# The sample streams of an attention stage follow each other every fourth unit in place of every sixth

## The chip, the cores and the metric

The kernel runs on one core of a Trainium2 chip. The metric is the time of one execution in microseconds of device time; of several runs the median counts.

## The reference

One layer of a streaming encoder. A combined input projection feeds two groups of heads, a retention mixer and an attention with a learned index; both go through an output projection, a normalization and a feed-forward block. There are two inputs: a prompt of 1024 frames, and 8 running streams ("samples") with 16 new frames each, which see 256 cached keys beside their own. The part that the change touches is the attention, for the prompt and for the samples alike:

```python
score = jnp.where(admissible[None], score, -jnp.inf)
sel_score, sel = lax.top_k(score, n_sel)
k_sel = gather(k, sel)
v_sel = gather(v, sel)
logits = jnp.einsum('bqgrd,bqkgd->bqgrk', qg, k_sel).astype(jnp.float32) * (HD ** -0.5)
logits = jnp.where(valid[:, :, None, None, :], logits + bias, -jnp.inf)
p = jax.nn.softmax(logits, axis=-1)
out = jnp.einsum('bqgrk,bqkgd->bqgrd', p.astype(v.dtype), v_sel)
```

The kernel doesn't gather. It adds a mask to the logits of all keys, so a key that isn't selected gets no weight.

## The kernel before

The kernel goes through index scores, retention, attention, output projection and the two halves of the feed-forward block. In each stage every engine has a program of its own, written out in order; the engines wait for each other through semaphores. So the order of an engine's instructions is the order in the code, and an instruction that waits holds everything behind it on its engine.

The attention stage (`attention_programs`, L1511) has 64 units, one for each of 8 tiles of 128 queries and 8 heads: unit u is tile u // 8, head u % 8. All engines loop over u. At unit u TensorE forms the logits of unit u (`qk_u`, L1957), transposes the probabilities of unit u-2 (`turn_u`, L1968) and multiplies those of unit u-3 with the values (`pv_u`, L1984). VectorE adds mask and bias and finds the largest value (`logits`, L1803 and L1809), ScalarE takes the exponential (`exps`, L1732) and copies the transposed probabilities out of the PSUM (`keeps`, L1741). A tile t has t + 1 blocks of 128 keys, so units become longer with t. At every eighth unit the queries of the next tile are turned (`queries_turn`, L1906).

The eight sample streams are woven into these units. Stream s has six steps, at six units in a row, and `stream_at(u, step)` (L1575) says which stream, if any, has that step at unit u:

- Step 0: TensorE waits for the stream's cached keys and values (`c_in`), then transposes the keys (`keys_turn`, L1912 and L1913); ScalarE copies them (`keep_keys`, L1708 and L1709).
- Step 1: TensorE forms the logits and adds the mask (`qk_s`, L1924 and L1926); VectorE reduces them (`logits_s`, L1770).
- Steps 2 and 3: ScalarE takes the exponential (`exp_s`, L1714); VectorE inverts the sum (`invert_s`, L1775).
- Step 4: TensorE transposes the probabilities (`turn_s`, L1932); ScalarE copies them (`keep_probs_s`, L1722 and L1724).
- Step 5: TensorE multiplies them with the values (`pv_s`, L1943); VectorE scales the result (`out_s`, L1782); SyncE stores it.

On TensorE the order in a unit is: turned queries, `qk_u`, `keys_turn`, `qk_s`, `turn_u`, `turn_s`, `pv_s`, `pv_u`. On ScalarE it is: kept queries, `keep_keys`, `keeps`, `exps`, `exp_s`, `keep_probs_s`. On VectorE the logits of the unit come first, then `logits_s`, `invert_s` and `out_s`.

Keys and values of a stream lie in `kp` and `vp`, which have two buffers each, buffer s % 2 for stream s. The first two streams are loaded ahead of the stage. After that SyncE's program (`sync`, L1654) does the following at a unit that holds step 5 of stream s:

```python
sp.wait_ge(s_o, s + 1)
for h in range(HEADS):
    sp.dma_start(mix[r0:r0 + NEW, 512 + 64 * h:576 + 64 * h],
                 os_[h * NEW:(h + 1) * NEW, s % 2, :]).then_inc(s_out[s % 2], 16)
if s + 2 < NS:
    caches_in(sp, s + 2)
```

`s_o` counts the outputs of `out_s`. The eight stores are L1676; `caches_in` (L1627) issues a load of 128 KB of keys and one of 128 KB of values (L1633), and both count on the semaphore for which `keys_turn` waits. On the same queue stand, in the order of the units, the query and key rows of the next tiles (`queries_in`, L1624 and L1625, at units 5, 13, 21 and so on), the output projection's weights (L1670, at units 8, 10, 16, 18, 24, 26, 32 and 34, which wait for GpSimd from unit 16 on) and the stores of a finished tile (L1683, at units 10, 18, 26 and so on).

The PSUM banks for transposes, stream logits and stream outputs are three, taken in turn; the list of their uses is built from `stream_at`, so it follows any change there.

Of the kernel before, what the change touches and what calls it, by code (L numbers as in the profile page):

```python
# [278 lines left out]


RING = 12
STREAM_START, STREAM_GAP = 2, 6


class WeightRing:
# [2972 lines left out]
```

## Time and profile before

| | before |
|---|---|
| median of 3 runs | 1518.24 us (1518.0 to 1518.44) |
| the profiled execution's own time | 1519.36 us |
| its span | 1517.6 us |
| TensorE busy | 1455.2 us, 96% of the span |
| VectorE, ScalarE, GpSimd busy | 66%, 50%, 53% |
| mean granted clock of TensorE | 0.987 |

A busy share is an average over all stages. What a change in the attention stage is worth is read from the rows of that stage, which lies between about 490 and 663 us.

### The profile page before, as it was taken

How to read it: one execution, taken by the hardware profiler on the slowest of the kernel's cores; microseconds unless marked ns; L12 is line 12 of the kernel's file. 1: busy time of each engine (PE TensorE's matmuls, PEld its weight loads, DVE VectorE, ACT ScalarE, POOL GpSimd, SP SyncE). 2: the span in 40 equal slices, each digit the busy share in tenths (PEclk: the TensorE clock that was granted, in tenths of full speed). 3: DMA queues.
4: the chain of work that ended last, by engine and by line, in shares of the span. 5: the costliest groups of instructions: out<-in, count | busy, mean ns of one | idle time of the engine just before them, and what ended most of it. 6: DMA issues, size and time to landing. Idle time of an engine off the chain costs nothing.

```text
span 1517.6 us, 23208 instructions
## 1 busy us (share of the span) xinstructions
PE 1455.2 (96%) x7764; PEld 1214.9 (80%) x7764; DVE 1001.4 (66%) x1892; ACT 755.1 (50%) x1550; POOL 807.0 (53%) x685
## 2 busy tenths in 40 slices
PE   7998999999998899999999999999999999999995
PEld 6986787877777789988878888888887888888874
DVE  5368577777876654423459666566669777777787
ACT  5467477777676777634343334333344332332332
POOL 3310356656542343002456556546558977877888
PEclk9999899999999999999999999999999999999998
DMA  7310312121108451114322433433356444444344
GB/s 229 86 37 12 101 34 66 51 54 39 51 29 180 109 145 34 44 63 153 122 96 87 163 110 136 163 124 144 142 193 238 164 139 147 156 139 155 106 157 166
DMA packets 123886, 172.99 MB, mean 114 GB/s; under 512 B 46424, under 2 KB 95992, under 8 KB 121592
## 3 DMA queue, kind: packets, MB, share of 16 engines
q1 hardware_dynamic: 119840, 140.02, 30.1%
q10 hardware_dynamic: 3928, 31.48, 5.1%
q8 instruction: 63, 1.03, 0.3%
q14 instruction: 55, 0.45, 0.1%
HBM read 119.59 MB, written 51.88 MB: 113 GB/s over the span
## 4 chain that ended last, share of the span: by engine, by line
PE 60%; DVE 3%; POOL 3%; ACT 2%; issue 2%; SPq 1%; DMA 0%; POOLq 0%; ACTq 0%; DVEq 0%
PE wide L389 10%; PE wide L390 10%; PE wide L391 10%; PE paired L389 7%; PE paired L390 7%; PE paired L391 7%; PE paired L1984 4%; PE wide L1957 2%; PE paired L1968 2%; POOL acc L3044 1%; POOL acc L3053 1%; PE paired L2272 0%; DVE qT L1837 0%; DVE ob_mT_lo L2360 0%; SPq L1625 0%
## 5 line engine op out<-in xcount | busy, mean ns | idle before, releaser
L2169 POOL TENSOR_TENSOR wu_lo<-raw_u,wu_hi 128x512 fp32r<-128x512 f32 x64 | 97.0, 1529 | 148.1 <-ACT wu_hi L2164 148.1
L389 PE MATMUL paired<-w_hi,aT_hi 128*128 128x512 f32 x320 | 132.2, 413 | 1.4 <-PEq L424 1.4
L391 PE MATMUL paired<-w_hi,aT_lo 128*128 128x512 f32 x320 | 126.4, 395 | 0.0
L390 PE MATMUL paired<-w_lo,aT_hi 128*128 128x512 f32 x320 | 126.0, 394 | 0.0
L374 POOL TENSOR_TENSOR w_lo<-stage,w_hi 128x512 fp32r<-128x512 f32 (+1 forms) x50 | 64.4, 1303 | 99.2 <-ACT w_hi L369 99.2
L3083 DVE TENSOR_TENSOR acc<-wide,acc 128x512 f32<-128x512 f32 x116 | 79.5, 687 | 45.4 <-PE wide L391 45.2
L1070 ACT ACTIVATE spare<-scores,sl_key 128x768 bf16<-128x768 f32 (+2 forms) x96 | 100.1, 1043 | 11.3 <-DVE sl_key L1176 3.8
L389 PE MATMUL paired<-aT_hi,wu_hi 128*128 128x512 f32 x240 | 95.1, 396 | 1.5 <-DVE acc L3083 1.2
L2169 POOL TENSOR_TENSOR wu_lo<-w_sum,wu_hi 128x512 fp32r<-128x512 f32 x60 | 96.5, 1638 | 0.0
L390 PE MATMUL paired<-aT_lo,wu_hi 128*128 128x512 f32 x240 | 93.6, 390 | 0.0
L391 PE MATMUL paired<-aT_hi,wu_lo 128*128 128x512 f32 x240 | 93.6, 390 | 0.0
L3013 POOL TENSOR_TENSOR aT_lo<-t_sum,aT_hi 128x512 fp32r<-128x512 f32 x52 | 78.1, 1531 | 27.2 <-ACT aT_hi L2918 27.2
L1199 DVE TENSOR_SCALAR_CACHE_REDUCE spare<-scores,sl_key 128x384 bf16<-128x384 f32 (+3 forms) x128 | 86.8, 678 | 4.6
L1867 POOL TENSOR_TENSOR near<-bias,scores 128x2048 f32<-128x2048 f32 (+1 forms) x8 | 34.3, 4292 | 91.1 <-DVE mn L1809 69.9
L2936 ACT ACTIVATE aT_hi<-w_all 128x1792 fp32r<-128x1792 f32 x16 | 27.2, 1698 | 98.2 <-PE wide L391 98.2
L2586 DVE TENSOR_TENSOR f_out<-f_out 128x512 f32<-128x512 f32 (+1 forms) x48 | 49.4, 1029 | 39.8 <-ACT f_out L2563 32.6
L389 PEld LDWEIGHTS paired<-w_hi,aT_hi 128*128 128x128 f32 x320 | 60.4, 189 | 18.1 <-issue 5.0
L1984 PE MATMUL paired<-vt,pT 128*128 128x64 f32 x576 | 72.8, 272 | 1.0 <-ACT pT L1741 0.6
L1984 PEld LDWEIGHTS paired<-vt,pT 128*128 128x128 f32 x576 | 69.8, 193 | 2.4 <-ACT pT L1741 1.2
L391 PEld LDWEIGHTS paired<-w_hi,aT_lo 128*128 128x128 f32 x320 | 60.2, 188 | 14.0
L390 PEld LDWEIGHTS paired<-w_lo,aT_hi 128*128 128x128 f32 x320 | 60.4, 189 | 11.4
L2336 POOL TENSOR_SCALAR ob_st<-ob_st 128x1 f32<-128x1 f32 x18 | 3.4, 191 | 124.0 <-ACT ob_junk L2297 112.5
(393 smaller groups left out, 4732.3 us busy)
## 6 DMA issues: line engine op xcount, KB each, us to landing
f_scratch<-f_out ACTq DMA_DIRECT2D x15, 1984.0 KB, 6.1
w_all<-f_scratch SPq DMA_DIRECT2D x32, 896.0 KB, 4.8
raw_u<-in_w_up SPq DMA_DIRECT2D x16, 1024.0 KB, 5.4
raw_d<-in_w_down SPq DMA_DIRECT2D x16, 1024.0 KB, 7.1
stage<-in_w_in SPq DMA_DIRECT2D x32, 256.0 KB, 3.4
stage<-mix_scratch SPq DMA_DIRECT2D x9, 512.0 KB, 4.0
h_scratch<-ob_h SPq DMA_DIRECT2D x9, 512.0 KB, 2.9
fn_h<-h_scratch SPq DMA_DIRECT2D x9, 512.0 KB, 7.8
```

The source lines that it names most:

```text
L374: self.nc.gpsimd.tensor_tensor(lo, raw, hi.bitcast(F32), ALU.subtract).then_inc(self.lo_done, 1)
L389: nc.tensor.matmul(out, lhs[0], rhs[0], start=first, stop=False, skip_group_check=onto)
L390: nc.tensor.matmul(out, lhs[0], rhs[1], start=False, stop=False, skip_group_check=onto)
L391: return nc.tensor.matmul(out, lhs[1], rhs[0], start=False, stop=last, skip_group_check=onto)
L1070: nc.scalar.activation(act_junk[:, 0:P * (t + 1)], score[t][:], ACT.Sign, scale=-1.0, bias=limit, accum_out=c_sum[:, n:n + 1]).then_inc(sl ...
L1199: nc.vector.tensor_scalar(dve_junk[:, 0:cells.shape[1]], cells, limit, None, ALU.is_ge, ALU.add, accum_out=c_sum[:, n:n + 1]).then_inc(sl_ ...
L1867: nc.gpsimd.tensor_tensor(near[:, t % 2, :, 2 * P - w:], bias[:, :, 2 * P - w:], repeated(mask[t][:, P * (t + 1) - w:], 1, HEADS), ALU.add ...
L1984: mm = nc.tensor.matmul(po[:, h * HD:(h + 1) * HD], pT[:, n % 3, k * P:(k + 1) * P], vt[:, k0 + k, 64 * g:64 * g + 64], start=(k0 + k == 0 ...
L2169: self.nc.gpsimd.tensor_tensor(self.room.wu[1][:, s], self.source(i), self.room.wu[0][:, s].bitcast(F32), ALU.subtract).then_inc(self.lo_d ...
L2586: nc.vector.tensor_tensor(out, x, y, op).then_inc(marked, 1)
L3013: op = nc.gpsimd.tensor_tensor(s[1][:, n], x[:, n], s[0][:, n].bitcast(F32), ALU.subtract)
L3083: nc.vector.tensor_tensor(cells, bank, cells, ALU.add).then_inc(added, 1)
```

## The change

`STREAM_GAP` is the distance of two streams in units. It goes from 6 to 4. Stream s then begins at unit 2 + 4s in place of 2 + 6s, and ends at 7 + 4s in place of 7 + 6s; the last stream ends at unit 35, in the fifth tile, in place of unit 49, in the seventh. Steps 4 and 5 of stream s come to stand in the same units as steps 0 and 1 of stream s + 1. The load of the caches of stream s + 2 stands at unit 4s + 7 on SyncE, and the step that needs them at unit 4s + 10; before, these were 6s + 7 and 6s + 14.

```diff
 RING = 12
-STREAM_START, STREAM_GAP = 2, 6
+STREAM_START, STREAM_GAP = 2, 4
```

`STREAM_GAP` is used in one place:

```python
def stream_at(u, step):
    s, rest = divmod(u - STREAM_START - step, STREAM_GAP)
    return s if rest == 0 and 0 <= s < NS else None
```

## Rows read from the trace of the kernel before

**Rows 1.** Windows: us; busy (count) of PE, PEld, DVE, ACT, POOL; clock; DMA share; GB/s.

```profile
499.00:662.00 163.00, 155.04 (x1263) 139.85 (x1262) 82.10 (x282) 117.09 (x284) 46.07 (x15) 1.00 0.29 76
500.00:510.00 10.00, 8.45 (x71) 7.11 (x72) 6.70 (x27) 6.97 (x29) 4.56 (x1) 1.00 0.04 8
```

**Rows 2.** Waits of PE, 485 to 665 us: us in total, times, longest.

```profile
PE paired L1943 <- issue: 2.1, 3, 1.0
```

**Rows 3.** Timeline of SyncE's DMA queue: start, us, line, DMA, count.

```profile
504.28 3.57 SPq L1676 DMA_DIRECT2D mix_scratch<-os  x8
...
509.17 0.47 SPq L1633 DMA_DIRECT2D vp<-in_cache_v  x1
...
511.83 4.23 SPq L1625 DMA_DIRECT2D krow<-out  x1
516.11 4.20 SPq L1676 DMA_DIRECT2D mix_scratch<-os  x8
...
539.83 3.67 SPq L1676 DMA_DIRECT2D mix_scratch<-os  x8
...
544.03 0.47 SPq L1633 DMA_DIRECT2D vp<-in_cache_v  x1
...
551.72 4.79 SPq L1676 DMA_DIRECT2D mix_scratch<-os  x8
...
557.04 0.47 SPq L1633 DMA_DIRECT2D vp<-in_cache_v  x1
```

**Rows 4.** DMA issues, 485 to 670 us: count, KB each, median us to landing.

```profile
vp<-in_cache_v SPq DMA_DIRECT2D x6, 128.0 KB, 2.3
```

**Rows 5.** Timeline of DVE: start, us, line, out<-in [idle before, its releaser].

```profile
496.49 0.44 DVE L1770 CUSTOM_DVE_ANT_0 ps<-paired,bias_s 128x272 f32<-128x272 f32 x1 [1.12 <-PE paired L1926]
...
503.96 0.28 DVE L1782 TENSOR_SCALAR os<-paired,rdens 128x64 f32<-128x64 f32 x1 [1.01 <-PE paired L1943]
```

**Rows 6.** Timeline of PE in the attention stage, same columns.

```profile
503.13 0.45 PE L1943 MATMUL paired<-vp,psT 128*64 128x64 f32 x8 [0.99 <-issue]
...
503.77 0.43 PE L1984 MATMUL paired<-vt,pT 128*128 128x64 f32 x2
...
506.43 0.36 PE L1957 MATMUL wide<-kT_hi,qT 128*128 128x256 f32 x1
...
513.95 0.27 PE L1912 MATMUL paired<-ident,kp 128*128 128x128 f32 x1
...
514.39 0.56 PE L1984 MATMUL paired<-vt,pT 128*128 128x64 f32 x4
514.75 0.36 PE L1957 MATMUL wide<-kT_hi,qT 128*128 128x256 f32 x1
...
515.16 0.68 PE L1924 MATMUL paired<-kpT,aqS 64*64 64x272 f32 x4
...
516.22 0.56 PE L1984 MATMUL paired<-vt,pT 128*128 128x64 f32 x4
...
518.62 0.42 PE L1957 MATMUL wide<-kT_hi,qT 128*128 128x384 f32 x1
...
540.88 1.00 PE L1984 MATMUL paired<-vt,pT 128*128 128x64 f32 x8
...
547.38 0.48 PE L1957 MATMUL wide<-kT_hi,qT 128*128 128x512 f32 x1
```

**Rows 7.** Timeline of PE behind two idle times of about 2 us.

```profile
425.74 0.49 PE L1457 MATMUL wide<-qkT 64*128 64x128 f32 x4 [1.95 <-ACT qkT L1036]
...
429.91 0.43 PE L391 MATMUL paired<-w_hi,aS_lo 128*128 128x512 f32 x1
...
795.10 1.92 PE L2272 MATMUL paired<-ident,ob_x 128*128 128x128 f32 x8 [2.27 <-DVE ob_x L2375]
...
798.53 0.43 PE L390 MATMUL wide<-aT_lo,wu_hi 128*128 128x512 f32 x1
```

**Rows 8.** Windows, columns as in rows 1; the clock is the third number from the end.

```profile
492.00:498.00 6.00, 5.84 (x26) 4.69 (x26) 3.65 (x17) 3.09 (x14) 0.00 (x0) 0.50 0.46 88
796.00:798.00 2.00, 2.00 (x8) 1.81 (x7) 1.25 (x2) 1.88 (x3) 0.00 (x0) 0.50 0.64 227
```

## The prediction

> **What bounds the kernel now.** I read the windows first. Between 499 and 662 us, the stretch of the attention units, TensorE is busy 155.04 of 163 us, and even in its idlest ten, 500 to 510, 8.45 [rows 1]. The reader is to see that there is little to win here, at most 8 us of idle time, and that a delay of TensorE is handed on. Then the waits of TensorE: the ones that belong to the sample streams are those of L1943 (the products of a stream's probabilities with its values), 2.1 us in three waits [rows 2]. Nowhere in this stretch does TensorE wait for a DMA. The caches of stream s+2 are loaded into the buffer of stream s, and in the kernel before there is time enough for that: stream 0's output is written at 503.96 [rows 5], and stream 2's first transposes stand in row 513.95 [rows 6]. Last I read the queue of SyncE, which issues these loads, because the change moves the streams closer together and leaves this queue as it is.
>
> **Part 1, the streams' arithmetic.** Nothing is added or removed: the same transposes, products, copies and DMAs run, 2.3 streams' worth of them earlier. A stream's own work on TensorE is 0.22 us for two key transposes (four transposes take 0.44 from row 513.95 to 514.39), 0.84 for its logits (515.16 to 516.22 less two transposes), 0.33 for three transposes of probabilities and 0.64 for the products with the values (503.13 to 503.77): 2.03 us [rows 6]. TensorE is the bound of this stretch, so moving this work saves nothing by itself. What can be saved is the wait ahead of L1943, 2.1 us in all, since the logits of stream s+1 (0.84 us) now stand ahead of the products of stream s and cover it. On VectorE the reduction of stream s+1's logits, 0.44 us, comes ahead of stream s's output, which takes 0.28 [rows 5]; nothing else waits behind it.
>
> **Part 2, the way back of a cache buffer.** This is where the time goes. With step 5 of stream s at unit 4s+7, SyncE waits for the output, issues eight stores, then the key and the value load of stream s+2, and TensorE needs these at step 0 of stream s+2, unit 4s+10. Formerly the units were 6s+7 and 6s+14. So three units must cover the way back in place of seven. Its price is in SyncE's rows: from the first store to the value load 4.89 us for stream 0 (504.28 to 509.17), 4.20 at the shortest (539.83 to 544.03), 5.32 at the longest (551.72 to 557.04), six in all with a mean of 4.64 [rows 3]; then 2.3 us until the load has landed [rows 4]. That is a way back of 6.5 to 7.6 us, and I take 7.0. (If landing counts from the end of an issue, 0.47 us come on top; the upper end of the range takes that in.)
>
> What has three units to offer? From the products at the end of unit 15, row 516.22, to unit 18, row 518.62, is 2.40 us; with unit 18's own logits (0.41) and without the 0.47 us that the output needs, 2.3 us. That is the shortest. The longest is from 540.88 (unit 27) to 547.38 (unit 30): 6.5 plus 0.55 less 0.47, 6.6 us [rows 6]. The other three, read alike without the stream instructions in them, have about 4.0, 4.9 and 3.7. All are under 7.0: **TensorE waits for the caches of streams 2 to 7**, 3.0, 4.6, 2.1, 3.3 and 0.4 us from the second wait on. It stands at the head of its own queue there, so the units' transposes and products behind it wait too, and then ScalarE and VectorE, which feed on them.
>
> **The sum at full clock.** From the key transposes of stream s+2 to the output of stream s+1 lie, on TensorE: 0.22 (keys), 0.22 (unit's transposes), 0.33, 0.36 (514.39 to 514.75), 0.41 (logits of the next unit, 514.75 to 515.16), 0.84, 0.22, 0.64, and then 0.47 to the end of the output (503.96 plus 0.28, less 503.77) [rows 5, 6]: 3.7 us in the second tile. In the fourth tile twice as many blocks are transposed and the logits are twice as wide: about 4.5. Over the five rounds this is 20 us. A round is that plus the way back, so the five rounds from stream 2's keys to stream 7's take 5 x 7.0 + 20 = 55.0 us. The first begins at 504.24 plus 0.44 for the reduction now ahead, plus 7.0: 511.7, where the kernel before came by at 506.43 plus 0.3, so the first wait is 5.0 us. Stream 7's keys are then at 566.7 in unit 30, whose logits ended at 547.9 before: 18.8 us late. By then two streams more are done, which is 4.1 us of TensorE's work, and some 0.9 of the former waits are no longer ahead. So the end of the stage moves by 18.8 - 4.1 - 0.9 = **13.8 us**. Bounds: 0.5 less in each of six ways back gives 10.8, and 0.6 more gives 17.4.
>
> **The clock.** TensorE idles 2 to 5 us before each of five rounds. The trace has two idle times of that size after dense work: 1.95 us before 425.74 and 2.27 before 795.10. After either, products of 512 columns take longer until 429.91 and 798.53, that is for 4.2 and 3.4 us [rows 7], and the granted clock at 796 to 798 is 0.50, the 1.2 GHz level; from 492 to 498, behind an interrupted start of this very stage, it is 0.50 for 6 us [rows 8]. Work done for 3.4 to 4.2 us at half the clock costs 1.7 to 2.1 us, for 6 us it costs 3.0. All of this falls on the chain from the keys to the next output, which sets the length of a round, so it isn't hidden. Five times 2.0 is **10 us**; ends 0 and 15. I take 2.0 because the work behind each wait is dense, as in rows 7.
>
> The Trainium skill ("TensorE: Matmul & The Clock Gate", section "HAM oscillation — how this bites in real kernels") says that a loop which waits for a DMA in each pass begins each pass on the lower clock and pays for it every time. By that rule the sum is 23.8, and without it 13.8; rows 7 agree with it for gaps of 2 us.
>
> **Carried over.** The stages behind are bound by TensorE and start with it, so 13.8 + 10 = 23.8 us pass through. The profiled execution has a span of 1517.6 us and took 1519.36; the sum makes these 1541.4 and 1543.2. The median of the runs lies 1.1 lower, 1518.24, and becomes **1542.0 us**.
>
> **Rivals.** *The way back fits into three units.* Place: SyncE's queue at L1676 and L1633. It decides below about 2.3 us of way back, where all waits vanish; then only the covered wait of L1943 and its kin is left as a gain, 2.1 to 3 us, and the time is 1515.5. Against it: eight stores alone take 3.6 to 4.8 us to issue [rows 3]. For it: only that the kernel before never waits there. Chance 0.05, half of it faster and half within 0.2%, which is about what a measurement of this kernel can tell from no change. The Trainium skill ("DMA: Bandwidth & Descriptors", section "Anatomy of one DMA — SWDGE (gpsimd) path") gives a DMA of the GpSimd path some 50 ns of dispatch and a fixed 2.0 us; were that so for SyncE, ten issues and one landing would be an estimated 2.8 us, nearly this rival. The trace has 4.2 to 5.3 us for what the page makes half a microsecond, and the measurement decides.
>
> *The waits come, but the clock stays up*: 13.8 us, 1532.0. It decides where the waits are shorter than those of rows 7. For it: the granted clock is 1.00 from 500 to 510, though TensorE idles 0.99 us before 503.13 in there [rows 1, 6]. Against: both 2 us gaps in rows 7, and only one of my five waits is near 2. Chance 0.17.
>
> *The queue is also held by other loads.* The issue of a tile's key rows took 4.23 us at 511.83 and the stores behind it began only at 516.11 [rows 3]. If it or a weight load falls ahead of an output in two or three rounds, each costs up to 4 us: about 10 us more, 1552. The loads of the output weights (L1670) wait for GpSimd besides, at units 16, 18, 24 and 26, and the outputs of units 19 and 27 stand behind them. In the new order all these stand right behind a cache load, while the queue would idle until the next output, so I count nothing for them and give the rival 0.08.
>
> **How the numbers follow.** Forecast 0.70, rivals 0.05, 0.17 and 0.08. The range goes from the waits alone with short ways back (10.8 us, 1529) to the forecast with the long stretch of low clock and longer ways back (13.8 + 15 + 3.6 and a little over, 1552). Slower by over 0.2% holds 0.95, within 0.2% 0.025, faster 0.025.
>
> **What would show it.** In the profile after: TensorE's key transposes (L1912) wait for a DMA into kp or vp, five or six times, longest at streams 2 and 4, some 18 us in total (5.0 + 3.0 + 4.6 + 2.1 + 3.3 + 0.4); the rows from a stream's output to its buffer's next key transposes show about 7 us each time; the granted clock falls to 0.5 behind these waits; the waits of L1943 shrink; from the sixth tile on the units are as before, without stream instructions, and all stages behind are shifted by one amount. The forecast is wrong if no such wait shows, or if the low clock doesn't follow it.

## The result and the profile after

The changed kernel takes 1541.51 us (median of 4 runs, 1540.33 to 1542.03) where the kernel before takes 1518.34 (median of 4 as well, one run more than in the table ahead). The ratio is 1.0149 with a 95% interval of 1.0137 to 1.0162: **22.6 us slower**. The profiled execution took 1540.33 us, with a span of 1538.5.

All of it arises in the attention stage. From the stage's first product with keys to the first transpose of the output stage pass 194.3 us, from 490.26 to 684.58. In the kernel before these two stand at 491.71 and 662.80, 171.1 us apart (start, us, line, what; in brackets the idle time before and what ended it):

```profile
491.71 0.47 PE L1957 MATMUL wide<-kT_hi,qT 128*128 128x128 f32 x1 [1.91 <-DVE kT_lo L1837]
...
662.80 1.04 PE L2272 MATMUL paired<-ident,stage 128*128 128x128 f32 x8
```

The same two are the first and the last line of TensorE's timeline after, with the key transposes of streams 2 to 7 between them:

```profile
490.26 0.33 PE L1957 MATMUL wide<-kT_hi,qT 128*128 128x128 f32 x1 [1.91 <-DVE kT_lo L1837]
...
509.13 0.45 PE L1912 MATMUL paired<-ident,kp 128*128 128x128 f32 x1 [4.96 <-DMA vp<-in_cache_v]
...
522.30 0.34 PE L1912 MATMUL paired<-ident,kp 128*128 128x128 f32 x1 [1.30 <-DMA vp<-in_cache_v]
...
534.23 0.45 PE L1912 MATMUL paired<-ident,kp 128*128 128x128 f32 x1 [3.88 <-DMA vp<-in_cache_v]
...
548.74 0.27 PE L1912 MATMUL paired<-ident,kp 128*128 128x128 f32 x1
...
560.40 0.45 PE L1912 MATMUL paired<-ident,kp 128*128 128x128 f32 x1 [3.45 <-DMA vp<-in_cache_v]
...
574.78 0.27 PE L1912 MATMUL paired<-ident,kp 128*128 128x128 f32 x1
...
684.58 1.04 PE L2272 MATMUL paired<-ident,stage 128*128 128x128 f32 x8
```

Four of the six loads let TensorE wait, 13.6 us together, where the kernel before has no such wait in row 513.95 [rows 6]. The waits of the products with the values, the one row of [rows 2], are no longer among TensorE's longest. The waits of TensorE, 485 to 700 us (total, times, longest):

```profile
PE paired L1912 <- DMA vp<-in_cache_v: 13.6, 4, 5.0
PE paired L1968 <- DVE qT L1837: 2.8, 6, 0.9
```

The way back of a buffer can be read from VectorE's output to the key transposes in three steps. First VectorE's outputs of streams 0 and 1, then SyncE's queue behind them, which answers to [rows 3, 5]:

```profile
502.43 0.28 DVE L1782 TENSOR_SCALAR os<-paired,rdens 128x64 f32<-128x64 f32 x1 [0.39 <-PE paired L1943]
514.92 0.28 DVE L1782 TENSOR_SCALAR os<-paired,rdens 128x64 f32<-128x64 f32 x1 [1.10 <-PE paired L1943]
```

```profile
502.74 3.57 SPq L1676 DMA_DIRECT2D mix_scratch<-os  x8
506.41 0.40 SPq L1633 DMA_DIRECT2D kp<-in_cache_k  x1
506.85 0.47 SPq L1633 DMA_DIRECT2D vp<-in_cache_v  x1
...
515.23 3.95 SPq L1676 DMA_DIRECT2D mix_scratch<-os  x8
519.28 0.40 SPq L1633 DMA_DIRECT2D kp<-in_cache_k  x1
519.72 0.47 SPq L1633 DMA_DIRECT2D vp<-in_cache_v  x1
```

Stream 0's output ends at 502.71, the stores take until 506.3, the value load is issued at 506.85, and at 509.13, 2.28 us behind that, TensorE goes on: 6.4 us. Stream 1: from 515.20 to 522.30, 7.1 us. The other two that end in a wait are 6.5 and 7.3 us.

Behind three of the waits TensorE then works at half its clock, the 1.2 GHz level, and behind the short one for part of the time. Windows (columns as in [rows 1]; the clock is the third number from the end):

```profile
509.00:519.00 10.00, 9.87 (x50) 8.22 (x51) 2.19 (x8) 4.51 (x16) 0.00 (x0) 0.50 0.35 129
522.00:526.00 4.00, 3.70 (x17) 2.85 (x17) 0.43 (x2) 2.65 (x8) 0.18 (x1) 0.57 0.80 159
534.00:547.00 13.00, 12.77 (x63) 10.64 (x63) 3.47 (x13) 5.64 (x17) 0.98 (x1) 0.53 0.36 115
560.00:567.00 7.00, 6.60 (x28) 4.88 (x28) 2.06 (x7) 2.20 (x7) 0.99 (x1) 0.51 0.55 179
```

Summed over windows of 1 us, TensorE is busy for 38.3 us at the lower level between 485 and 720 us, against 6.2 us in the kernel before (that stretch is in [rows 8]). Over the whole stage TensorE is busy 177.4 us in place of 163.0 for the same instructions, and idle 17.0 us in place of 8.1. So of the 23.2 us that the stage grew, 14.4 are slower work and 8.8 are idle time: the waits of 13.6 us partly took the place of idle time that the kernel before has elsewhere.

### The profile page after: what moved, and what is told of

It reads as the page before. It is cut to its first block, busy times and chain, and to the rows that moved or that the text cites. A ratio compares the mean times of both kernels' runs of the same rounds, so it can differ in the third digit from the quotient of the medians.

```text
span 1538.5 us, 23208 instructions
## 1 busy us (share of the span) xinstructions
PE 1468.1 (95%) x7764; PEld 1224.7 (80%) x7764; DVE 1003.7 (65%) x1892; ACT 756.1 (49%) x1550; POOL 805.9 (52%) x685
## 4 chain that ended last, share of the span: by engine, by line
PE 59%; DVE 4%; POOL 3%; SPq 2%; issue 2%; ACT 2%; DMA 1%; POOLq 0%; DVEq 0%; ACTq 0%
PE wide L389 10%; PE wide L391 9%; PE wide L390 9%; PE paired L389 7%; PE paired L390 7%; PE paired L391 7%; PE paired L1984 4%; PE paired L1968 2%; PE wide L1957 2%; POOL acc L3044 1%; SPq L1676 1%; DMA vp<-in_cache_v 1%; POOL acc L3053 1%; PE paired L1924 0%; POOL wu_lo L2169 0%
## 5 line engine op out<-in xcount | busy, mean ns | idle before, releaser
L1984 PE MATMUL paired<-vt,pT 128*128 128x64 f32 x576 | 76.3, 280 | 0.0
L1984 PEld LDWEIGHTS paired<-vt,pT 128*128 128x128 f32 x576 | 73.9, 202 | 1.0
L1741 ACT ACTIVATE pT<-paired 128x512 f32<-128x512 f32 (+3 forms) x96 | 46.5, 487 | 53.6 <-PE paired L1968 35.3
```

The source lines that it names most:

```text
L1741: nc.scalar.activation(pT[:, n % 3, 0:w], bank_of("probs", n)[:, 0:w], ACT.Copy).then_inc(p_kept, 1)
L1984: mm = nc.tensor.matmul(po[:, h * HD:(h + 1) * HD], pT[:, n % 3, k * P:(k + 1) * P], vt[:, k0 + k, 64 * g:64 * g + 64], start=(k0 + k == 0 ...
```

## The experiments

**The loads ahead of the stores.** If the stores in SyncE's queue make the way back long, it must become short when the loads go first. They may: they need the stream's products to be done, not its output.

```diff
             if s is not None:
+                if s + 2 < NS:
+                    caches_in(sp, s + 2)
                 sp.wait_ge(s_o, s + 1)
...
-                if s + 2 < NS:
-                    caches_in(sp, s + 2)
```

> Gap 4; SyncE issues the loads of stream s+2 ahead of the eight stores of stream s, as soon as stream s's products are done. Theory (the way back of a cache buffer is the cause, and 3.6 to 4.8 us of it are the stores in front of the loads): the way back shrinks from about 6.8 us to about 3, the waits at the key transposes shrink from 13.6 us in four to under 2 us in one or two, the granted clock stays at 1.00, and the time is that of the kernel before or a little under it: 1516 to 1520 us. Rival A (the streams' steps standing in the same units is what costs, through banks, ScalarE or VectorE): little changes, 1535 to 1541. Rival B (the loads land late because of other transfers, not because they are issued late): waits of about 2 to 4 us stay, 1528 to 1538.

Measured: 1522.87 us, ratio 1.0017 (1.0002 to 1.0032) where the changed kernel had 1.0149. So what stood in front of the loads, the stores and the 0.47 us that the output needs, is the main part of the loss. But the time is 3 us above the expected range, and the waits didn't shrink to under 2 us. TensorE's waits, the landing times of all eight value loads (us, lowest, median, highest), SyncE's queue and TensorE behind the longer wait show why:

```profile
PE paired L1912 <- DMA vp<-in_cache_v: 4.7, 2, 3.6
```

```profile
DMA to landing us min/median/max: 2.1/4.1/6.8
```

```profile
508.81 0.90 SPq L1670 DMA_DIRECT2D stage<-in_w_out  x2
509.75 0.44 SPq L1683 DMA_DIRECT2D mix_scratch<-spare  x1
510.29 0.38 SPq L1633 DMA_DIRECT2D kp<-in_cache_k  x1
510.71 0.51 SPq L1633 DMA_DIRECT2D vp<-in_cache_v  x1
```

```profile
517.66 0.45 PE L1912 MATMUL paired<-ident,kp 128*128 128x128 f32 x1 [3.56 <-DMA vp<-in_cache_v]
```

The loads of stream 3 go out behind 1 MB of output weights and a tile of 256 KB, and TensorE gets them at 517.66, 7 us after the value load's issue. With the stores in front, the loads come later and land in 2.3 to 2.6 us; that they miss these transfers there is read from the order, not tested. So rival B's mechanism holds for this one wait, though not its time. The 3.6 us are followed by about 11 us of work at the lower level; with those at the stage's start, which the kernel before has too, it is 17.6 us.

**The weights out of the way too.** The same kernel, with loads and splits of the output weights four units later.

```diff
-    w_load_at = {8 * t - 16 + 2 * k: ...
-    w_split_at = {8 * t - 10 + 2 * k: ...
+    w_load_at = {8 * t - 12 + 2 * k: ...
+    w_split_at = {8 * t - 6 + 2 * k: ...
```

> Gap 4, the loads of stream s+2 ahead of the stores, and the loads and splits of the output weights four units later, so that the first pair no longer stands between the loads of streams 2 and 3. Theory (with the loads first, stream 3's loads landed late, 7 us after issue, because 1 MB of output weights was ahead of them in the DMA rings): the wait of 3.6 us at stream 3 falls under 1 us, the low clock behind it vanishes, time 1516 to 1520 us, 3 to 5 us under the kernel with the loads first alone. Rival (the landing was late for another cause, as the stores of stream 0): the wait stays at 3 us or more and the time at 1521 to 1525.

Measured: 1526.80 us, ratio 1.0057 (1.0039 to 1.0075): a miss in time, above the theory's range and the rival's, and half a hit in the mechanism. The wait at stream 3 is gone, as it should be, but one of 1.63 us has come at stream 4, ahead of whose load a weight load now stands. Stream 2 waits 1.94 us in place of 1.09, though nothing stands right ahead of its loads in either run: 3.3 us pass from its value load's issue to the key transposes (503.57 to 506.85), and 2.4 in the run before (503.50 to 505.93). The copies of the weights also moved to where ScalarE prepares the next tile's queries:

```profile
PE paired L1968 <- DVE qT L1837: 7.6, 6, 2.0
PE paired L1912 <- DMA vp<-in_cache_v: 3.7, 3, 1.9
```

That the query wait grew because of the copies is argued from their order, not shown by a run of its own. What the run shows is that the late landing at stream 3 went when the transfers ahead of it were moved; why stream 2's load landed later than in the run before stays open.

**Three buffers.** A third buffer for keys and values, in a part of `spare` that is free in this stage, takes the way back out of the loop; the stores stay in front. (The load of stream 2 now goes out at unit 4; its lines, the buffer's definition and the semaphores' counts are left out here.)

```diff
-        for dst, name in ((kp, "cache_k"), (vp, "cache_v")):
+        for dst, name in ((keys_of(s), "cache_k"), (values_of(s), "cache_v")):
...
-                if s + 2 < NS:
-                    caches_in(sp, s + 2)
+                if s + 3 < NS:
+                    caches_in(sp, s + 3)
```

> Gap 4; keys and values of the streams have three buffers in place of two, so a load has seven units instead of three; the stores stay in front. Theory: no TensorE wait on kp or vp is left, clock 1.00, time 1514 to 1518 us, that is the kernel before less the 2 to 3 us of waits at the streams' last products. Rival A (steps in the same units cost by themselves): 1525 to 1541, with waits at other instructions.

Measured: 1518.29 us, ratio 0.9985 (0.9971 to 0.9999), at the upper end of the expected range. No wait on a load is left, so the distance of the streams costs nothing by itself. TensorE's largest waits, without those at the start of the stage and of the output stage:

```profile
PE paired L1976 <- DVE qT L1845: 4.7, 7, 1.1
...
PE paired L1940 <- ACT pT L1749: 1.8, 3, 1.1
```

(The lines are shifted by eight: these are the units' transposes and the streams' transposes, L1968 and L1932 before.) Since 2 us are little, it ran again:

> Three buffers at gap 4 once more, with five rounds, since 2 us are to be told from nothing: theory (the streams' own waits of 2 to 3 us go, covered by the next stream's logits) 0.9975 to 0.9995 of the kernel before; rival (nothing is won by the distance itself) 0.9995 to 1.0010.

Measured: 1516.61 us, ratio 0.9973 (0.9962 to 0.9984), so **this version is faster than both kernels**: by the two ratios it lies 2.3 and 4.1 us below the kernel before. And the same buffers at the old distance:

> Gap 6 as in the kernel before, three buffers for the streams' keys and values. Theory: the kernel before has no wait on these loads, so a third buffer brings nothing: within 1.5 us of the kernel before. If it is 2 us or more faster, the 2 us that gap 4 with three buffers won come from the buffers and not from the gap.

Measured: 1519.34 us, ratio 1.0005 (0.9994 to 1.0016). The buffers alone bring nothing that can be told from noise. There the waits of [rows 2] are unchanged, 2.1 us in three; at distance 4 they are not among the waits.

Not all of the gain is these covered waits. At distance 4 the units' transposes wait 4.7 and 5.0 us in the two profiles, against 2.1 at distance 6 and 2.8 in the kernel before, and the streams' transposes 1.8. The stage, measured as above, takes 170.1 and 169.9 us in place of 171.1: about 1 us less. For the rest there is only an estimate. The mean granted clock of the executions is 0.9875 and 0.9882 in the two runs with three buffers at distance 4, and 0.9868 and 0.9862 in the kernel before beside them; these 0.0007 and 0.0020, over a span of some 1517 us, are worth at most 1.1 and 3.0 us. Where in the kernel the clock was higher isn't shown. One place may be the waits that are covered now: in the profile at distance 6, TensorE works at the lower level behind one of them, with a mean clock of 0.52 from 502 to 509 us (the stage takes 174.0 us there), while behind the same wait in the kernel before (503.13, [rows 6]) the clock stayed at 1.00.

```profile
502.06 0.69 PE L1951 MATMUL paired<-vp,psT 128*64 128x64 f32 x8 [0.99 <-issue]
```

**Distance 5.** A dose between the two, with two buffers and the stores in front.

```diff
-STREAM_START, STREAM_GAP = 2, 4
+STREAM_START, STREAM_GAP = 2, 5
```

> Gap 5, two buffers, stores in front: a cache buffer has five units for its way back. Theory (a race between the way back, 6.4 to 7.3 us, and the units between): from unit 7 to unit 12 lie only about 4.6 us, so stream 2 waits about 2 us and one short stretch of low clock follows; from unit 12 to 17 lie about 7.2 us and later more, so no other wait. Time 1517 to 1523 us, nearly all of the loss gone at once. Rival (the loss grows evenly with the nearness of the streams): about half of it stays, 1528 to 1532 us.

Measured: 1522.29 us, ratio 1.0023 (1.0014 to 1.0033).

```profile
509.33 0.45 PE L1912 MATMUL paired<-ident,kp 128*128 128x128 f32 x1 [2.07 <-DMA vp<-in_cache_v]
...
543.99 0.30 PE L1912 MATMUL paired<-ident,kp 128*128 128x128 f32 x1 [0.71 <-DMA vp<-in_cache_v]
```

The wait of 2 us at stream 2 is there as computed, and one of 0.7 at stream 5, which wasn't. So the loss is a race between two times and not a slope: one unit less in the distance costs little, a second unit costs the rest.

**The stores twice.** The opposite dose: eight more stores, to a scratch tensor nobody reads, ahead of each pair of loads. (The definition of the tensor and the semaphores' counts are left out here.)

```diff
+                for h in range(HEADS):
+                    sp.dma_start(again[s, h], os_[h * NEW:(h + 1) * NEW, s % 2, :]).then_inc(s_out[s % 2], 16)
                 if s + 2 < NS:
```

> Gap 4; each stream's eight stores are issued twice, the second time to a scratch tensor that nobody reads, ahead of the loads of stream s+2. Theory: each of six ways back is 3.4 to 3.8 us longer, all six end in a wait, and two more stretches of low clock follow: 1541 plus 19 to 27, 1560 to 1568 us. Rival (the stores in front don't matter, the landing does): 1541 to 1546.

Measured: 1574.32 us, ratio 1.0346 (1.0317 to 1.0376), about 30 us above the changed kernel by the ratios. All six loads make TensorE wait, the stores' own time doubles, and the low clock becomes the rule: 73.2 us of work at the lower level, a mean clock of 0.67 from 505 to 612 us.

```profile
PE paired L1915 <- DMA vp<-in_cache_v: 31.6, 6, 10.0
```

```profile
503.76 4.72 SPq L1677 DMA_DIRECT2D mix_scratch<-os  x8
508.52 3.66 SPq L1680 DMA_DIRECT2D again_scratch<-os  x8
```

```profile
505.00:612.00 107.00, 73.48 (x399) 59.02 (x398) 28.43 (x117) 42.37 (x121) 26.33 (x9) 0.67 0.27 75
```

The price of a store, some 0.46 us (3.66 for eight), is as forecast. The total is 6 us above my range. The waits grew by 18.0 us, to 31.6, less than the six times 3.4 to 3.8 that I had counted; the work at the lower level grew by 34.9 us, to 73.2, where I had counted only two more stretches.

**The waits filled with work.** To tell the clock from the waits, TensorE transposes the identity before each of five waits, into the bank that the keys overwrite afterwards.

```diff
             bank = claim("keys", s)
+            for _ in range({2: 40, 3: 20, 4: 36, 5: 14, 6: 26}.get(s, 0)):
+                nc.tensor.transpose(bank[:, 0:P], ident[:], ident[:])
             pe.wait_ge(c_in[s % 2], 32 * (s // 2 + 1))
```

> Gap 4, the way back unchanged; ahead of the key transposes of streams 2 to 6 TensorE does 40, 20, 36, 14 and 26 transposes of the identity that nobody reads (about 0.11 us each), so that it works while it would wait. Theory (about 10 us of the 23 are the low clock behind the waits): the granted clock stays at 1.00 behind these places, the waits proper are under 1.5 us each, and although TensorE does 15 us more work the time falls to 1528 to 1534 us. Rival (the low clock is hidden in the next way back and costs nothing): time unchanged, 1540 to 1543. Rival (extra work only adds): over 1545.

Measured: 1532.46 us, ratio 1.0079 (1.0053 to 1.0105). TensorE does 15.7 us more work (4.53, 2.35, 4.09, 1.69 and 3.00), still waits 3.8 us (2.17 of them at stream 2, above the 1.5 expected), and the kernel is about 10 us faster by the ratios. The clock is 1.00 from 499 to 570 us, where the filled waits lie:

```profile
504.21 4.53 PE L1912 MATMUL paired<-ident 128*128 128x128 f32 x40
510.91 0.33 PE L1914 MATMUL paired<-ident,kp 128*128 128x128 f32 x1 [2.17 <-DMA vp<-in_cache_v]
518.95 2.35 PE L1912 MATMUL paired<-ident 128*128 128x128 f32 x20
522.40 0.33 PE L1914 MATMUL paired<-ident,kp 128*128 128x128 f32 x1 [1.10 <-DMA vp<-in_cache_v]
```

```profile
499.00:570.00 71.00, 64.02 (x544) 54.87 (x543) 30.38 (x126) 42.10 (x130) 23.03 (x7) 1.00 0.41 109
```

**The changed kernel again, and both on one chip.** Twice more the changed kernel ran as it is, the second time beside the filled one.

> The changed kernel as it is, beside the others of this call, so that they can be compared on one chip: 1.013 to 1.017 of the kernel before, 1539 to 1545 us.

Measured: 1535.93 us, ratio 1.0120 (1.0102 to 1.0137), below what I expected. The waits are those of before in sum; the clock isn't. Behind a wait of 2.66 us at 556.18 it stays up, and behind one of 1.49 us at 521.56 too:

```profile
PE paired L1912 <- DMA vp<-in_cache_v: 13.8, 5, 5.1
```

```profile
556.18 0.30 PE L1912 MATMUL paired<-ident,kp 128*128 128x128 f32 x1 [2.66 <-DMA vp<-in_cache_v]
```

```profile
556.00:562.00 6.00, 5.82 (x49) 4.62 (x50) 2.17 (x8) 3.44 (x10) 1.57 (x1) 1.00 0.68 219
```

In this profile 22.1 us of work are at the lower level, in place of 38.3.

> The changed kernel again, on the chip of the next two runs. The two profiles so far have the same waits at the key transposes, 13.6 and 13.8 us, but 38 and 22 us of work at the lower clock, and differ by 5.6 us in time. Theory (waits cost the same everywhere, the clock behind them not): waits of 13 to 15 us again, and a time between 1.011 and 1.016 of the kernel before, higher with more work at the lower clock.

> The filled waits again, beside the unfilled ones on one chip: the difference is what the lower clock costs there. Theory: the time is 1.007 to 1.009 of the kernel before as it was, since no low clock is left that could vary, so 5 to 12 us under the run beside it. Rival (the difference between the two was one of chips): less than 3 us under it.

Measured: 1540.21 us, ratio 1.0133 (1.0113 to 1.0153), and 1532.98, ratio 1.0087 (1.0068 to 1.0105). On one chip the filled waits are 7.2 us faster, so the low clock costs about that there. The filled kernel came out alike on two chips; the unfilled one ranged from 1.0120 to 1.0149 in its three measurements. In this profile its waits are 15.7 us in four, above the 13 to 15 expected, with one of 6.3 among them, and 24.9 us of work are at the lower level. So the waits vary too, and time doesn't follow the low clock alone.

## Why the prediction was right

**The sum.** 1542.0 was forecast and 1541.51 came. The filled kernel lets the two terms be measured apart. The term of the waits at full clock, 13.8 us, came out at 12.0 and 13.2 (the ratios 1.0079 and 1.0087 of 1518 us); the stage alone, 186.9 and 186.5 us in the two profiles against 171.1, has 15.8 and 15.4. The term of the clock, 10 us, is what the unfilled kernel takes more: 7.0 us by the ratios on one chip, and 5.0 to 10.6 over all pairs of the two kernels' ratios. So the first term was right in size, and the second lies at the upper end of what was measured. That the total fits to half a microsecond is luck, since the same kernel lay between 1.0120 and 1.0149.

**The way back of a buffer.** Forecast 7.0 us, 6.5 to 7.6; measured 6.4, 7.1, 6.5 and 7.3, mean 6.8. The open question, whether landing counts from the start or the end of an issue, is settled: 2.3 to 2.6 us lie between the start of the value load's issue and the key transposes, so the 0.47 us were not on top. That the stores are the reason is shown from both sides, by the loads ahead of them (1.0017) and the stores twice (1.0346), and that the loop through the buffer is the cause by the third buffer (0.9985 and 0.9973).

**The single waits.** Here the steps were off. Forecast were 5.0, 3.0, 4.6, 2.1, 3.3 and 0.4 us, 18.4 together; the changed kernel shows 5.0, 1.3, 3.9, none, 3.5 and none, 13.6. The sum of 18.4 belongs to a kernel at full clock, and there it held: the filled kernel spends 15.7 us on the filling and waits 3.8. In the real one the work at the lower clock didn't end with the next output, as I took it, but ran on into the units that the way back must be covered with (10 us behind 509, 12 behind 534), and these cover more of it when they are slow. I had said of the low clock that "it isn't hidden"; part of it is hidden in the next wait. Against that, three of the four stretches were longer than those of [rows 7]: 9.9, 3.4, 12.1 and 6.4 us of work, where the prediction read 4.2 and 3.4 from the products (the granted clock puts both at 3.4). These two errors cancelled in part, and the term came out near the forecast.

**Rivals.** That the way back fits into three units: no, four waits. On SyncE's queue eight further stores took 3.66 us, 0.46 each. The Trainium skill's figure of some 50 ns of dispatch ("DMA: Bandwidth & Descriptors", section "Anatomy of one DMA — SWDGE (gpsimd) path") is for the GpSimd path, and these rows show that it can't be carried over to SyncE's. That the clock stays up: not so in the changed kernel; the filled kernel is this case by construction, and lies 12.0 and 13.2 us above the kernel before where 13.8 was worked out. The Trainium skill ("TensorE: Matmul & The Clock Gate", section "HAM oscillation — how this bites in real kernels") tells of a measured kernel in which each pass of a loop starts on the lower clock behind its DMA wait. The four windows after the change agree, with 0.50 to 0.57, but not every execution does: the wait of 2.66 us in the repeated run wasn't followed by the lower clock. That other loads hold the queue: not in the changed kernel, where the issues behind a load were done before the next output, as the timeline of SyncE shows; but the transfers of such loads held up a landing as soon as the stores no longer stood between (loads first). I had looked at the queue's issue and not at the landing.

**What the overlap saves.** Forecast 2.1 to 3 us when nothing waits; the kernel with three buffers is 2.3 and 4.1 us below the kernel before by its two ratios, and the same buffers at distance 6 are level with it. The size fits, the mechanism only in part: the waits of L1943 are gone as forecast, but other waits came in their place, so the stage is only about 1 us shorter. The rest may be the clock, by the estimate above; that isn't shown.

## What to carry to other kernels

When steps of a double-buffered stream move closer together, time the way back of a buffer, from the last reader to the landed load, with everything that stands ahead of the load in its queue, and hold it against the shortest stretch of work between, not the mean: here 7 us against the 2.3 to 6.6 that the prediction read. A wait of the engine that bounds the stage can cost more than its length, when the clock falls behind it; filling the wait with useless work shows how much, here 5.0 to 10.6 us over five waits. If the shift is wanted, the buffer has to come back earlier or there must be one more: with a third buffer the same change took 2.3 and 4.1 us off this kernel.

## What was not expected of the hardware

- The lower clock lasted longer behind three of the waits here than in the rows of the kernel before: 9.9, 12.1 and 6.4 us of work behind waits of 5.0, 3.9 and 3.5 us, against 3.4 us by the granted clock behind each of the idle times of 2.0 and 2.3 us in [rows 7].
- Whether it comes isn't settled by the length of a wait alone. It followed waits of 1.30 us (changed kernel, 522.30) and 0.99 us (three buffers at distance 6, 502.06), and didn't follow one of 2.66 us (the changed kernel again, 556.18). What decides between them stays open.
- A value load of 128 KB landed in 2.2 us in the median of the changed kernel's six, with only the small stores and its key load right ahead of it, and took up to 6.8 us behind 1.25 MB of other transfers (loads first).
